# A hybrid attention and SSD encoder layer: in the head loop, GpSimd takes the convolution, the decays' exponents, the sum of squares and the two gates

## The reference

```python
proj = rmsnorm(x) @ w_in                       # q, k, v, gates z_attn and z_ssm, xbc, dt
o = dilated_attention(q, k, v, rel_bias)       # 16 heads x 128, all pairs of tokens with a bias table
attn_out = rmsnorm(o, attn_norm_g) * silu(z_attn)
xbc = silu(conv5(xbc) + conv_b)                # centred depthwise convolution, 5 taps, per channel
a_cs = cumsum(dt * a)                          # per chunk of 128 tokens, both directions
decay = exp(where(causal, a_cs[l] - a_cs[s], -inf))
y_diag = (C B^T * decay) @ (x * dt)            # within a chunk; y_off carries the state of other chunks
y = (y_diag + y_off + d_skip * x) * silu(z_ssm)
mix = concat(attn_out, group_rmsnorm(y)) @ w_out
y_out = x + rmsnorm(mix, post_norm_g)
```

## Time and profile before

| | us |
|---|---|
| median of 2 runs (lowest, highest) | 2484.73 (2483.93, 2485.53) |
| the profiled execution | 2484.6 |
| its span | 2482.8 |
| TensorE busy in the span | 2455.8 |
| VectorE busy | 1590.8 |
| ScalarE busy | 915.0 |
| GpSimd busy | 0.2 |

### The profile page before, as it was taken

The page is one execution under the profiler, slowest core; times in us unless marked ns, Lnnn a source line. Parts: engine busy times, 40 slices in busy tenths (PEclk is TensorE's granted clock), DMA queues, the critical chain, the costliest instruction groups (busy, mean ns, idle before and its releaser), DMA issues.

```text
span 2482.8 us, 36702 instructions
## 1 busy us (share of the span) xinstructions
PE 2455.8 (99%) x13956; PEld 2330.9 (94%) x13956; DVE 1590.8 (64%) x2304; ACT 915.0 (37%) x1510; POOL 0.2 (0%) x4
## 2 busy tenths in 40 slices
PE   7999999999999999999999999999999999999998
PEld 6999999999999999999999999999999888888887
DVE  5566955555555555554888878887888654544447
ACT  6333333333333333333544454455445321111122
POOL 0000000000000000000000000000000000000000
PEclk9999999999999999999999999999999999999999
DMA  4234333333333333345454645554554322222225
GB/s 160 77 110 152 115 94 93 98 103 100 97 105 95 99 93 93 101 138 187 149 154 136 219 141 153 184 170 143 177 163 130 123 96 92 93 95 92 93 86 186
DMA packets 287792, 309.34 MB, mean 125 GB/s; under 512 B 12918, under 2 KB 230198, under 8 KB 284775
## 3 DMA queue, kind: packets, MB, share of 16 engines
q1 hardware_dynamic: 254519, 202.39, 26.5%
q10 hardware_dynamic: 33200, 106.02, 12.7%
HBM read 254.73 MB, written 60.98 MB: 127 GB/s over the span
## 4 chain that ended last, share of the span: by engine, by line
PE 98%; ACT 1%; DVE 1%; DMA 0%; issue 0%; SPq 0%; DVEq 0%; ACTq 0%
PE ps L863 34%; PE ps L662 23%; PE ps L936 20%; PE ps L642 8%; PE ps L821 2%; PE ps L788 2%; PE ps L755 2%; PE ps L771 1%; PE ps L831 1%; PE ps L597 0%; PE ps L795 0%; PE ps L762 0%; PE ps L676 0%; PE ps L804 0%; PE ps L844 0%; PE ps L945 0%
## 5 line engine op out<-in xcount | busy, mean ns | idle before, releaser
L863 PE MATMUL ps<-h_hi,w_hi 128*128 128x384 f32 x928 | 311.0, 335 | 1.1 <-issue 1.1
L863 PE MATMUL ps<-h_hi,w_lo 128*128 128x384 f32 x928 | 310.6, 335 | 0.0
L863 PE MATMUL ps<-h_lo,w_hi 128*128 128x384 f32 x928 | 310.5, 335 | 0.0
L936 PE MATMUL ps<-h_hi 128*128 128x512 f32 x752 | 293.5, 390 | 0.0
L936 PE MATMUL ps<-h_lo,h_hi 128*128 128x512 f32 x752 | 292.6, 389 | 0.0
L936 PE MATMUL ps<-h_hi,h_lo 128*128 128x512 f32 x752 | 292.5, 389 | 0.0
L1898 DVE TENSOR_TENSOR w_lo<-raw_qk,w_hi 128x512 fp32r<-128x512 f32 x232 | 160.2, 691 | 194.1 <-ACT w_hi L1315 193.1
L662 PE MATMUL ps<-h_hi,w_hi 128*128 128x384 f32 x1088 | 283.2, 341 | 0.0
L662 PE MATMUL ps<-h_lo,w_hi 128*128 128x384 f32 x1088 | 277.0, 335 | 0.0
L662 PE MATMUL ps<-h_hi,w_lo 128*128 128x384 f32 x1088 | 277.0, 335 | 0.0
L1025 ACT ACTIVATE w_hi<-w_raw 128x512 fp32r<-128x512 f32 x184 | 115.1, 628 | 411.9 <-PE ps L662 275.4
(11 more groups left out here) (265 smaller groups left out, 4240.1 us busy)
## 6 DMA issues: line engine op xcount, KB each, us to landing
w_raw<-in_w_in SPq DMA_DIRECT2D x184, 256.0 KB, 3.6
raw_qk<-in_w_in SPq DMA_DIRECT2D x87, 512.0 KB, 3.9
stage<-in_w_out SPq DMA_DIRECT2D x31, 1024.0 KB, 5.0
stage<-loc_scr ACTq DMA_DIRECT2D x16, 1536.0 KB, 7.0
stage<-zx_scr ACTq DMA_DIRECT2D x46, 384.0 KB, 8.5
stage<-in_w_in SPq DMA_DIRECT2D x29, 512.0 KB, 4.1
u_scr<-stage ACTq DMA_DIRECT2D x32, 384.0 KB, 2.7
zx_scr<-w_raw SPq DMA_DIRECT2D x29, 384.0 KB, 2.3
```

Source lines behind the costliest of these rows:

```text
L863: ins = nc.tensor.matmul(ps[:, bank, 0:HALF_T], w, h(k), start=(start and kk == 0 and q == 0), stop=(last and kk == KC - 1 and q == 2), sk ...
L936: last = nc.tensor.matmul(ps[:, bank, :], m[par][:, k * T + t * P:k * T + (t + 1) * P], w[slot][:, k * NBW:(k + 1) * NBW], start=(k == 0 a ...
```

## The change

GpSimd gets a program of its own for the head loop: for each head it subtracts the columns' part from the decays and clips them (`decay_exponents`), adds the square of the attention's output to `osq_sum`, multiplies the attention's output with its gate, convolves x of the next head (each further tap is now two instructions, a product into a buffer `tap_x` and a sum, where VectorE has one), and multiplies y with its gate. VectorE no longer does these. Three waits are new: ScalarE waits for `conved` before it writes the transposed probabilities (the new buffer `tap_x` lies in their space), GpSimd starts a convolution only after the product of probabilities and v of the head before, and in the last head VectorE waits for `decay_arg` before its step 2 (it then overwrites the columns' values).

```diff
@@ -221,14 +223,13 @@
+        tap_x = stage[:, PT_AT + PAIRS * P:PT_AT + PAIRS * P + T + 4]
...
@@ -1240,6 +1242,7 @@
                                              bias=nmx[:, PCH + t:PCH + t + 1],
                                              accum_out=lsum[:, PCH + t:PCH + t + 1]).then_inc(probs_exp, 1)
                 if a is not None and s == 2:
+                    act.wait_ge(conved, a + 1)
                     for b in range(PCH):
                         act.wait_ge(pt_ready, 4 * a + b + 1)
                         nc.scalar.activation(pT_hi[:, b * SEQ:(b + 1) * SEQ], ps[:, 4 + b, :], ACT.Copy
@@ -1477,6 +1480,69 @@
                     nc.scalar.activation(fin_rms[:, t:t + 1], fin_mean[:, t:t + 1], ACT.Sqrt).then_inc(fin_root, 1)
+        @block.gpsimd
+        def _(pool):
+            count = [0]
+            def did(ins):
+                ins.then_inc(pool_seq, 1)
+                count[0] += 1
+            def settle():
+                pool.wait_ge(pool_seq, count[0])
+            def convolve_xs(a):
+                pool.wait_ge(xs_in, 32 * a + 32)
+                if a:
+                    pool.wait_ge(osq_added, a)
+                W = T + 4
+                did(nc.gpsimd.tensor_scalar(conv[:, 0:W], xs_raw[:, 0:W], conv_cols[:, a:a + 1], convb_cols[:, a:a + 1],
+                                            ALU.mult, ALU.add))
+                for k in range(1, CONV_W):
+                    settle()
+                    did(nc.gpsimd.tensor_scalar(tap_x, xs_raw[:, k:k + W], conv_cols[:, 24 * k + a:24 * k + a + 1], None,
+                                                ALU.mult))
+                    settle()
+                    ins = nc.gpsimd.tensor_tensor(conv[:, 0:W], conv[:, 0:W], tap_x, ALU.add)
+                    if k < CONV_W - 1:
+                        did(ins)
+                    else:
+                        ins.then_inc(conved, 1)
+            def decay_exponents(a):
+                pool.wait_ge(decay_in, 16 * a + 16)
+                dv = decay.rearrange("p (r n) -> p r n", n=P)
+                did(nc.gpsimd.tensor_tensor(dv, dv, loc_cols[:, 24 * a:24 * a + 24].unsqueeze(2).broadcast_to([P, 24, P]),
+                                            ALU.subtract))
+                settle()
+                nc.gpsimd.tensor_scalar(decay, decay, EXP_MAX, None, ALU.min).then_inc(decay_arg, 1)
+            pool.wait_ge(cols_read, 2)
+            pool.wait_ge(loc_read, 2)
+            pool.wait_ge(pads, 3)
+            pool.wait_ge(osq_zeroed, 1)
+            convolve_xs(0)
+            for a in range(HEADS):
+                decay_exponents(a)
+                pool.wait_ge(o_sq, a + 1)
+                nc.gpsimd.tensor_tensor(osq_sum[:, :], osq_sum[:, :], sqT[:, 0:T], ALU.add).then_inc(osq_added, 1)
+                if a < HEADS - 1:
+                    pool.wait_ge(z_silu, 2 * a + 1)
+                else:
+                    pool.wait_ge(tile_out, tile_of(HEADS, 0) + 1)
+                nc.gpsimd.tensor_tensor(oT, oT, za, ALU.mult).then_inc(att_gated, 1)
+                if a < HEADS - 1:
+                    pool.wait_ge(pv_ready, 2 * a + 2)
+                    convolve_xs(a + 1)
+                pool.wait_ge(diag_read, a + 1)
+                if a < HEADS - 1:
+                    pool.wait_ge(z_silu, 2 * a + 2)
+                else:
+                    pool.wait_ge(tile_out, tile_of(HEADS, 1) + 1)
+                nc.gpsimd.tensor_tensor(y, y, zs, ALU.mult).then_inc(y_gated, 1)
         @block.vector
         def _(dve):
             seq = [0, 0]
@@ -1683,19 +1749,6 @@
             seq[:] = [0, start + BC_SEQ * (SSM_GROUPS - 1)]
             last_g = SSM_GROUPS - 1
-            def convolve_xs(a):
-                dve.wait_ge(xs_in, 32 * a + 32)
-                convolve(conv, xs_raw, lambda k: conv_cols[:, 24 * k + a:24 * k + a + 1], convb_cols[:, a:a + 1], conved)
-            def decay_exponents(a):
-                dve.wait_ge(decay_in, 16 * a + 16)
-                dv = decay.rearrange("p (r n) -> p r n", n=P)
-                tt(dv, dv, loc_cols[:, 24 * a:24 * a + 24].unsqueeze(2).broadcast_to([P, 24, P]), ALU.subtract)
-                settle()
-                nc.vector.tensor_scalar(decay, decay, EXP_MAX, None, ALU.min).then_inc(decay_arg, 1)
             def scaled_x(a):
                 dve.wait_ge(xt_out, 2 * a + 2)
                 dve.wait_ge(pv_ready, 2 * a + 1)
@@ -1767,7 +1820,6 @@
                             accum_out=mx[:, t:t + 1]).then_inc(biased, 1)
                     dve.wait_ge(biased, 6 * a + 4)
                     nc.vector.tensor_scalar(nmx[:, 0:4], mx[:, 0:4], -1.0, None, ALU.mult).then_inc(negmax, 1)
-                    convolve_xs(a)
                 if s == 1:
                     dve.wait_ge(probs_exp, 6 * a + 4)
                     did(nc.vector.reciprocal(rinv[:, 0:4], lsum[:, 0:4]))
@@ -1799,7 +1851,6 @@
                         dve.wait_ge(pt_out, 4 * a + b + 1)
                         nc.vector.tensor_tensor(pT_lo[:, part], ps[:, 4 + b, :], pT_hi[:, part].bitcast(f32), ALU.subtract
                                                 ).then_inc(pt_lo_done, 1)
-                    decay_exponents(a)
                     if i is None:
                         dve.wait_ge(u_first_in, 16)
                         nc.vector.tensor_tensor(ssum, u_first[0], u_first[0], ALU.mult).then_inc(usq_added, 1)
@@ -1807,14 +1858,6 @@
                     add_square_first(1)
                     add_square_first(2)
                 if s == 5:
-                    dve.wait_ge(o_sq, a + 1)
-                    tt(osq_sum[:, :], osq_sum[:, :], sqT[:, 0:T], ALU.add)
-                    settle()
-                    if i is not None:
-                        dve.wait_ge(z_silu, 2 * a + 1)
-                    else:
-                        dve.wait_ge(tile_out, tile_of(HEADS, 0) + 1)
-                    nc.vector.tensor_tensor(oT, oT, za, ALU.mult).then_inc(att_gated, 1)
                     weights_in_chunks(a)
                 if s == 6:
                     dve.wait_ge(xs_silu, a + 1)
@@ -1840,12 +1883,6 @@
                     dve.wait_ge(diag_ready, 2 * a + 2)
                     nc.vector.tensor_tensor(y, y, ps[:, 5:7, :].rearrange("p b n -> p (b n)")[:, 0:T], ALU.add
                                             ).then_inc(diag_read, 1)
-                    dve.wait_ge(diag_read, a + 1)
-                    if i is not None:
-                        dve.wait_ge(z_silu, 2 * a + 2)
-                    else:
-                        dve.wait_ge(tile_out, tile_of(HEADS, 1) + 1)
-                    nc.vector.tensor_tensor(y, y, zs, ALU.mult).then_inc(y_gated, 1)
             def block_sum(dst, kh, th):
@@ -2007,7 +2044,7 @@
             nc.vector.memset(xs_raw[:, 2 + SEQ:6 + SEQ], 0.0)
             nc.vector.memset(xs_raw[:, 6 + T:8 + T], 0.0).then_inc(pads, 1)
             dve.wait_ge(c2_out, 16 * NP)
-            did(nc.vector.memset(osq_sum[:, :], 0.0))
+            nc.vector.memset(osq_sum[:, :], 0.0).then_inc(osq_zeroed, 1)
             def iteration(i, ip, a):
                 for s in range(IT_CHUNKS):
@@ -2040,6 +2077,8 @@
                     m_hi[0][:, k * T:(k + 1) * T].bitcast(f32), ALU.mult, ALU.subtract).then_inc(m_lo_done, 1)
             for s in range(IT_CHUNKS):
+                if s == 2:
+                    dve.wait_ge(decay_arg, HEADS)
                 if s <= 1:
                     step(s, HEADS - 1, None)
                 if s + NCH < IT_CHUNKS:
@@ -2069,6 +2108,7 @@
                     if s < 4:
                         nc.vector.tensor_tensor(ssum, u_raw[:, 0:T], u_raw[:, 0:T], ALU.mult).then_inc(usq_added, 1)
                     else:
+                        dve.wait_ge(osq_added, HEADS)
                         copy(ssum, osq_sum[:, :]).then_inc(ssum_ready, 1)
                 elif s < 4:
                     dve.wait_ge(usq_done, (GRP - 1) * s + k)
```

More of the change, by code:

```diff
@@ L82 @@
 HT = HK * (T // 2)
-STAGE = 20112
+STAGE = 20120
 STRIP = SEQ + 3 * P
@@ L209, in encoder @@
         XW = T + 8
+        PROBS_AT = XW + 5 * T + STRIP
+        PT_AT = PROBS_AT + 4 * SEQ + 2 * DEC_SEQ
         xs_raw = carve(XW)
```

7 lines of the change are left out of this document (3 added, 4 removed).

## The result

The changed kernel takes 2621.32 us (2620.80 and 2621.85), 1.055 times the kernel before [1.054, 1.057]: 137 us more. The forecast was 2602, range 2487 to 2715. Its profiled execution took 2621.85 us, its span 2619.8.

A forecast was written before the change was run, and what follows sets the result against it. TensorE was taken to bound the head loop, without idle. A loss of 7.6 us in each of 15 heads (114 us) plus 3 in the last made 117 us over 2484.6: 2602 us, 4.7% slower, range 2487 to 2715.

The forecast's parts named there:

- What leaves VectorE is worth nothing: Per head 12.7 us of VectorE's 40.4 leave, gaining nothing, since TensorE has no idle; the head's tail starts 1.9 us earlier.
- Turns: VectorE instructions with two SBUF inputs and any GpSimd instruction shut each other out for the whole instruction; chance 0.62.
- GpSimd's price: GpSimd's 14 instructions per head cost a quarter above VectorE's rows, 19 us, so GpSimd does not bound by itself.
- The sum by it, 2760: Estimate of the whole time, about 2760 us, if GpSimd costs twice VectorE's rows.
- Place one: GpSimd's subtraction and clip of the decays hold up VectorE's `w_lo`; `pT_lo` comes late and TensorE loses 3.7 us per head.
- The rival of the late gate: Gate of y and decays' load late, so no loss at `pT_lo`; 0 to 3 us per head, 2487 to 2530; chance 0.08.
- The exponential: ScalarE's exponential of the decays starts at 1581.25; GpSimd hands them over at 1573.9, so nothing is lost.
- Place two: GpSimd's sum, gate and convolution meet VectorE in the head's tail; TensorE loses 3.9 us per head at scores or slot 7.
- elsewhere VectorE is ahead: Apart from `pT_lo` and the sum ahead of the next scores, VectorE's results were taken to be early enough for TensorE.
- The last head: VectorE waits for GpSimd's decays before step 2, so `pT_lo` comes late and TensorE loses 3.1 us once.
- The clock: Each loss of 4 us may bring 5 us at half clock, losing 2.5: 37 us more, no case of its own.
- The rival without turns: GpSimd reads beside VectorE without holding it up; only the last head waits, 2487 to 2493 us; chance 0.25.

The follow-up runs named there:

- ygate_only: Kernel before, with only the gate of y moved to GpSimd; convolution, decays, sum of squares and attention's gate on VectorE: 2486.2 us, 1.0008.
- The probe: Not the layer: VectorE and GpSimd run instructions on their own buffers, alone and together; GpSimd's 3072-column clip took 7.93 us with one operation, 2.75 with two.
- conv_dve: Changed kernel with the convolution back on VectorE in step 0: 2680.5 us, 1.079 times the kernel before.
- early_load: Changed kernel with ScalarE issuing the load of the next decays before the store of y: 2695.5 us, 1.085 times the kernel before.
- clip_two: Changed kernel with GpSimd's clip of the decays written with two operations instead of one: 2566.7 us, 1.033 times the kernel before.
- dec_dve: Changed kernel with the decays' subtraction and clip back on VectorE, without the last head's wait for them: 2551.8 us, 1.027 times the kernel before.
- all_two: As clip_two, with the four further taps of GpSimd's convolution also written with two operations: 2700.1 us, 1.085 times the kernel before.
- placed: As all_two, but GpSimd's subtraction waits for the first `pT_lo`, its sum of squares for both `v_lo`; last head's decays on VectorE: 2557.8 us, 1.030.

## Why the prediction came out

**What leaves VectorE is worth nothing:** right. ygate_only and the whole change show VectorE's relief without any gain; the forecast of a tail 1.9 us earlier was used up by the meetings.

**Turns:** right, and it carries the result. The probe shows it by itself, the rows of `w_lo`, `scaled_x` and line 1848 show it in their places. The class was drawn too small: one-input instructions on SBUF are shut out too, down to line 1822 on 4 columns (1.32 us for 0.17). The Trainium skill, "SBUF — State Buffer", section "Who interferes with whom", has the shared ports as exclusive for the length of an instruction, a VectorE instruction with at most one SBUF input (in its plain mode) outside of it, and `tensor_scalar` among those that can enter a mode that uses both ports. The traces agree (`v_lo` and `pT_lo`, from PSUM, keep 1.01 and 2.48 us, and the `tensor_scalar` forms are shut out), but for the clip, which let a two-input instruction in before its end.

**GpSimd's price:** mis-sized, 19 us per head against 42. The undisturbed rows of its 14 instructions add up to some 36 us (5.33, 7.93, 3 x 1.81, 0.98, 4 x 2.21, 4 x 1.81; an estimate), the rest is time held up. The quarter above VectorE's rows was a choice without a row; measured are 1.6 times for the subtraction, 2.0 for the sum of line 1506 (1916 against 945), and for one-operation forms 3.3 (2.22 against 0.68) and 4.7. The Trainium skill, "GPSIMD Engine Reference", section 3.1, has 4497 ns for a two-input sum of 2048 columns; the probe's row scaled to that length is 4.4 us (6.65 x 2048 / 3072, an estimate), so the trace agrees. The sum by it, 2760, is further off than 2602: in the same walk the better price makes both places dearer, and TensorE paid neither of them as walked.

**Place one (3.7 us per head in slot 3):** failed in its condition, that the load is in time. The rival of the late gate came true, 3.5 us late, and slot 3 paid nothing in heads 1 to 14. (The prediction has the gate due about 4 us after the sum; it had some 6, from 1602.38 - 48.70 = 1553.68 to the load's issue at 1560.14.) The mechanism is real: where the load is in time (conv_dve, early_load) slot 3 waits 8.8 and 9.0 us per head, at GpSimd's true prices.

**The exponential (nothing lost):** failed. With the load 3.5 us late and the clip 8.3 us long, the 7 us of room are gone: 24.6 us in slot 5, and 36.5 - 18.9 = 17.6 us of slot 6's waits by the late copies. clip_two gives both back. The late gate's own price, 0 to 3 us per head, missed this too.

**Place two (3.9 us per head, slot 7 and scores):** the sum is near, the place is not. Slot 7 and scores wait 17.6 us in all, 1.2 per head. I let the meetings begin behind `v_lo`; GpSimd starts at the square, on `scaled_x`, and slot 6 pays 36.5 us, 2.4 per head. I had not walked that stretch, and "elsewhere VectorE is ahead" hid how little room there was. Before, `v_lo` ended at 1589.36 and the product that slot 7 waits for at 1597.83; slots 6 and 7 began 2.0 and 1.0 us later:

```profile
1591.41 3.29 PE L821 MATMUL ps<-stage 128*128 128x128 f32 x28
1598.81 1.53 PE L831 MATMUL ps<-stage 128*64 128x128 f32 x24
```

**The last head (3.1 us):** mis-sized, 13.4, by GpSimd's prices; undoing it gives 16.5. Head 0 was missing: 10.3.

**The clock (2.5 us per head at the most):** right in size, 28.0 / 15 = 1.9. But the prediction kept it out of its sum.

So the loop's 114 us stand against 107.7 measured, but they are not the same things: 79.7 us of waits, most of them in other slots, and 28.0 us of clock, which the 114 did not hold. The direction rests on the turns alone. Its nearness is luck, between a price too low by half, a place that did not happen and terms that were left out. The rival without turns (2487 to 2493) fell with the probe. What stays open: what part of the clock's 28.0 us belongs to which wait, and which engine is let in first at a meeting.

## What to carry to other kernels

Two engines that take turns at a memory are one resource: before giving GpSimd work, list for each of its instructions what VectorE does in that time and which engine takes that result next, slot by slot, from the first moment that GpSimd may start. In a loop that TensorE fills, shorter or earlier is not better by itself. Less GpSimd work made two kernels faster (clip_two, dec_dve) and two slower (conv_dve, all_two), and the earlier load was among the slowest, because a late transfer had kept two instructions apart. If work must move, move what stands where the other engine is idle, as beside the gate of y, or reads PSUM, as in the probe, and expect nothing from it where the relieved engine was not the bound.

## What the hardware showed unexpectedly

- GpSimd's instruction with a scalar costs 7.93 us for 3072 columns with one operation and 2.75 with two; with a column 8.02 and 2.90.
- Turns go both ways: two of VectorE's 1536-column instructions (3.41 us) held a 2.22 us product of GpSimd for 5.40, though it was waiting when the second began. With placed, GpSimd's two-input sum did get in between two of them, which took 5.05 us for 3.41. What decides it no run here shows.
- A turn is not always the whole instruction: in the probe the clip ended 1.2 us after the two-input VectorE instruction that had waited for it.
- GpSimd's subtraction of 3072 columns in place, with one input broadcast along the columns, takes 5.33 us, the probe's sum with two full inputs 6.65. Which of the differences makes it no run here shows.
- A TensorE wait of some 4 us is followed by a granted clock of 0.74 over 10 us in which it has work throughout (all_two); after a wait of 2.75 us in the change, 0.50 stood over 2.1 us.
